# Attention jobs of a hybrid transformer kernel: full-array matmuls, streamed values, the window bias added on VectorE

## The reference

```python
qa = apply_axial_rope(rms_norm(qa...), cos, sin); ka = apply_axial_rope(rms_norm(ka...), cos, sin)
oa = gqa_attention(qa, ka, va) * silu(za)                 # A: 8 query heads, 2 key heads, head size 64
ob = neighbourhood_attention(qb, kb, vb, rpb) * silu(zb)  # B: 8 heads, window of columns + relative bias
mixed = sigmoid(ga) * (oa @ w_o_attn) + sigmoid(gb) * (ob @ w_o_na)
x = x + mixed @ w_out                                     # p = softmax(q k / 8 [+ bias]), out = p v
```

## Time and profile before

| | us |
|---|---|
| median of 3 runs | 1308.72 (1308.57 to 1310.63) |
| profiled execution | 1306.29 |
| its span | 1304.4 |
| PE / DVE / ACT / POOL busy in the span | 1232.6 / 873.0 / 633.6 / 258.6 |
| granted TensorE clock, mean | 0.978 |
| attention part of layer 0 (first score to last value) | 88.5 to 269.6 |
| attention part of layer 1 | 380.0 to 539.2 |

### The profile page before, as it was taken

The page is one execution under the profiler, slowest core; times in us unless marked ns, Lnnn a source line. Parts: engine busy times, 40 slices in busy tenths (PEclk is TensorE's granted clock), DMA queues, the critical chain, the costliest instruction groups (busy, mean ns, idle before and its releaser), DMA issues.

```text
span 1304.4 us, 23474 instructions
## 1 busy us (share of the span) xinstructions
PE 1232.6 (94%) x9420; PEld 1145.0 (88%) x9420; DVE 873.0 (67%) x1886; ACT 633.6 (49%) x960; POOL 258.6 (20%) x192
## 2 busy tenths in 40 slices
PE   6899997999899999989999999999999999999995
PEld 6888886779888887889999998988889999999995
DVE  5655443477655544687877668967784678777666
ACT  6544442246654443365444455447445465444453
POOL 0054553000055541000000004870066000000000
PEclk9999999899999999999999999999999999999998
DMA  6643313234643244145554554232456454554550
GB/s 231 149 158 117 111 66 81 49 112 168 152 165 118 97 101 94 65 162 210 194 182 157 197 185 178 107 133 92 144 145 164 150 201 165 191 194 146 198 207 33
DMA packets 47980, 188.09 MB, mean 144 GB/s; under 512 B 20856, under 2 KB 24184, under 8 KB 29312
## 3 DMA queue, kind: packets, MB, share of 16 engines
q1 hardware_dynamic: 47872, 186.58, 43.7%
HBM read 185.50 MB, written 1.06 MB: 143 GB/s over the span
## 4 chain that ended last, share of the span: by engine, by line
PE 73%; DVE 12%; DMA 6%; ACT 4%; issue 2%; SPq 2%; POOL 0%; DVEq 0%; ACTq 0%
PE line L1777 43%; PE result L1777 16%; DMA raw<-in_weights 4%; PE result L1927 4%; DVE w_lo L1098 3%; PE score L1879 3%; DMA rel<-in_rpb 2%; SPq L597 2%; PE turn L1900 1%; ACT w_hi L684 1%; PE score L1884 1%; PE score L2046 1%; DVE prod L1623 1%; DVE prod L1334 0%; DVE best L1622 0%
## 5 line engine op out<-in xcount | busy, mean ns | idle before, releaser
L667 POOL TENSOR_TENSOR w_lo<-raw,w_hi 128x512 fp32r<-128x512 f32 x184 | 257.8, 1432 | 669.0 <-ACT w_hi L684 669.0
L684 ACT ACTIVATE w_hi<-raw 128x2048 fp32r<-128x2048 f32 (+2 forms) x178 | 321.4, 1808 | 120.3 <-DMA raw<-in_weights 53.7
L1777 PE MATMUL line<-x_hi,w_hi 128*128 128x256 f32 (+1 forms) x1144 | 340.1, 297 | 15.3 <-DVE x_lo L1141 8.8
L1098 DVE TENSOR_TENSOR w_lo<-raw,w_hi 128x512 fp32r<-128x512 f32 (+2 forms) x528 | 323.3, 659 | 17.0 <-ACT w_hi L684 13.4
L1777 PE MATMUL line<-x_hi,w_lo 128*128 128x256 f32 (+1 forms) x1144 | 329.4, 288 | 0.0
L1777 PE MATMUL line<-x_lo,w_hi 128*128 128x256 f32 (+1 forms) x1144 | 329.0, 288 | 0.0
L1777 PEld LDWEIGHTS line<-x_hi,w_hi 128*128 128x128 f32 x1144 | 220.9, 193 | 27.9 <-issue 19.4
L1777 PEld LDWEIGHTS line<-x_lo,w_hi 128*128 128x128 f32 x1144 | 220.6, 193 | 0.9
L1777 PEld LDWEIGHTS line<-x_hi,w_lo 128*128 128x128 f32 x1144 | 221.0, 193 | 0.0
L1777 PE MATMUL line<-y_hi,w_hi 128*128 128x256 f32 (+1 forms) x688 | 205.1, 298 | 2.5 <-DVE y_lo L1149 1.7
L1777 PE MATMUL line<-y_lo,w_hi 128*128 128x256 f32 (+1 forms) x688 | 197.0, 286 | 0.0
(11 more groups left out here) (298 smaller groups left out, 2212.8 us busy)
## 6 DMA issues: line engine op xcount, KB each, us to landing
raw<-in_weights SPq DMA_DIRECT2D x145, 1024.0 KB, 4.8
raw<-in_weights SPq DMA_DIRECT2D x32, 704.0 KB, 4.0
rel<-in_rpb SPq DMA_DIRECT2D x64, 64.0 KB, 7.1
h<-in_tokens SPq DMA_DIRECT2D x2, 544.0 KB, 6.1
raw<-in_weights SPq DMA_DIRECT2D x2, 512.0 KB, 6.1
rbias<-bias_by_distance SPq DMA_DIRECT2D x8, 128.0 KB, 5.5
out<-wide SPq DMA_DIRECT2D x4, 256.0 KB, 2.2
consts<-in_consts SPq DMA_DIRECT2D x1, 832.0 KB, 6.8
```

The source lines that it names most:

```text
L667: pool.tensor_tensor(w_lo[:, u % CUT, at], raw[:, u % RAW, at], w_hi[:, u % CUT, at].bitcast(F32), ALU.subtract).then_inc(lo_pool, 1)
L684: act.activation(w_hi[:, v % CUT, first:n], raw[:, v % RAW, first:n], ACT.Copy).then_inc(hi_cut, 1)
L1098: dve.tensor_tensor(w_lo[:, u % CUT, at], raw[:, u % RAW, at], w_hi[:, u % CUT, at].bitcast(F32), ALU.subtract).then_inc(lo_cut, 1)
L1777: ins = pe.matmul(bank[:, 0:n], stay, move[:, first + k, 0:n], start=(k, m) == (0, 0), stop=(k, m) == (depth - 1, 2))
```

## The change

- Keys lie zero-padded in tiles of all 128 rows (`ka_half`, `kb` with a tile for each head), so scores use K = 128. Probabilities and value tiles are padded to 3 x 128 keys.
- B's queries are stored in reverse order within a tile, so the bias needs no flip matmul: DVE adds it to the scores in PSUM in the instruction that takes the (negated) maximum; Exp has scale -1.
- `values` has the turned probabilities as stationary operand (128 columns) and streams the 64 columns of `v`; the result is query by head, in one of two banks. DVE divides it by the sum there (64 columns in place of 272) and writes it to `head_out`; when both halves of a pair and tile are in, one transpose (`pair_out`) turns them to feature order. The jobs' order has the halves innermost.
- ACT alone copies the turned probabilities (384 columns).
- The walk is three steps longer (`TAIL`); steps 3, 7, 11, ... of the early part have no filler (six in layer 0, three in layer 1).
- The bias is loaded by head pair and query tile (4 DMAs) into a ring of 4; the later four chunks stand behind units that `rel_unit` picks.
- `rot` works on the raw line with the gain folded into its matrix (`rot_gain`); the norm is multiplied in last. `rot` moves to even lines.
- The dummy Ln that brought in an activation table becomes a load of a set by name.

```diff
-    a = [("A", c, half, t) for c in range(PAIRS) for half in range(2) for t in range(TILES)]
-    b = [("B", c, half, t) for c in range(PAIRS) for half in range(2) for t in range(TILES)]
+    a = [("A", c, half, t) for c in range(PAIRS) for t in range(TILES) for half in range(2)]
+    b = [("B", c, half, t) for c in range(PAIRS) for t in range(TILES) for half in range(2)]
...
+TAIL = 3
...
+def filler_at(i):
+
+    steps = len(JOBS[i]) + TAIL
+    blank = steps - len(FILLERS)
+    free = {3 + 4 * n for n in range(blank)}
+    at = [t for t in range(steps) if t not in free]
+    return {t: f for f, t in enumerate(at)}
...
+BIASES = [(c, t) for c in range(PAIRS) for t in range(TILES)]
+RING = 4
...
+def rel_unit(i, n):
+
+
+    c, t = BIASES[n - RING]
+    step = JOBS[i].index(("B", c, 1, t)) + 2
+    f = max(f for s, f in FILLER_AT[i].items() if s <= step)
+    return UNIT[(f"layer{i}", *FILLERS[min(f + 3, len(FILLERS) - 1)])] + RAW
...
+    single_bank = [stat_bank, result_bank[1]]
+    pair_bank = result_bank[0]
...
+    ka_half = a1.sb("ka_half", [2, TOK])
+    kb = a1.sb("kb", [HEADS, TOK])
+    head_out = a1.sb("head_out", [2, P])
     va = a1.sb("va", [3, P])
     vb = a1.sb("vb", [3, HEADS * HD])
-    rel = a1.sb("rel", [2, TILES, 2, SEQ])
+    rel = a1.sb("rel", [RING, 2, TOK])
+    rot_gain = a1.sb("rot_gain", [2, P])
...
-        def load_rel(i, c):
-
-
-            n = PAIRS * i + c
-            if n >= 2:
-
-                sp.wait_ge(score_done, SCORE[(f"layer{(n - 2) // PAIRS}", "B", (n - 2) % PAIRS, 1, TILES - 1)] + 1)
+        def load_rel(i, n):
+
+            k = len(BIASES) * i + n
+            c, t = BIASES[n]
+            if k >= RING:
+
+                j, (c0, t0) = (k - RING) // len(BIASES), BIASES[(k - RING) % len(BIASES)]
+                sp.wait_ge(maxed, JOB[j] + JOBS[j].index(("B", c0, 1, t0)) + 1)
             for half in range(2):
-                for r in range(ROWS):
-                    at = ((i * HEADS + 2 * c + half) * RPB_R + 7 - r) * RPB_C + WIN - GRID_W
+                for odd in range(2):
+                    at = ((i * HEADS + 2 * c + half) * RPB_R + 7 - 2 * t - odd) * RPB_C + WIN - GRID_W
                     src = bass.AP(rpb.tensor, at, [[1, GRID_W], [RPB_C, ROWS], [1, GRID_W]])
-                    dst = rel[(1 - r % 2) * GRID_W:(2 - r % 2) * GRID_W, n % 2, r // 2, half]
-                    sp.dma_start(dst.rearrange("p (r c) -> p r c", c=GRID_W), src).then_inc(rel_in[n % 2], 16)
+                    dst = rel[(1 - odd) * GRID_W:(2 - odd) * GRID_W, k % RING, half, 0:SEQ]
+                    sp.dma_start(dst.rearrange("p (r c) -> p r c", c=GRID_W), src).then_inc(rel_in[k % RING], 16)
...
-                for c, behind in enumerate((5, 6, 22, 24)):
-                    if u == STAGES[f"layer{i}"] + behind:
-                        load_rel(i, c)
+                for n in range(RING):
+                    if u == STAGES[f"layer{i}"] + 5 + n // 2:
+                        load_rel(i, n)
+
+                for n in range(RING, len(BIASES)):
+                    if u == rel_unit(i, n):
+                        load_rel(i, n)
...
+        pool.memset(prod2[:, :, TOK:3 * P], 0.0).then_inc(set_up, 1)
+        pool.memset(probs[:, :, TOK:3 * P], 0.0).then_inc(set_up, 1)
+        pool.memset(ka_half[:, :, :], 0.0).then_inc(set_up, 1)
+        pool.memset(kb[:, :, :], 0.0).then_inc(set_up, 1)
+        pool.memset(rel[:, :, :, SEQ:TOK], 0.0).then_inc(set_up, 1)
...
-            act.activation(warm[:, :], eps[:, :], ACT.Ln)
+            act.preload_act_table_set("natural_log_exp_and_others")
...
+                act.activation(probs[0:m, n % 2, 0:TOK], score_bank[s % 2][0:m, 0:TOK], ACT.Exp,
+                               bias=top[0:m, n % 2, 0:1], scale=-1.0 if job[0] == "B" else 1.0,
+                               accum_out=total[0:m, n % 4, 0:1]).then_inc(exped, 1)
...
-            def head_norm(n):
-                dst = ka[:, :] if n == 0 else qa[:, n - 1, 0:W]
-                g = operand(f"k_gain{i}") if n == 0 else q_gain[:, i:i + 1]
-                r = rstd_of((name, "head", n), W if n else TOK)
-                dve.scalar_tensor_tensor(dst, dst, g, r, ALU.mult, ALU.mult).then_inc(normed, 1)
...
+                dve.wait_ge(raw_head, 5 * i + n + 1)
+                dve.scalar_tensor_tensor(prod[:, 0, 0:w], dst, g, const("cos")[:, 0:w], ALU.mult, ALU.mult)
                 dve.wait_ge(rot_done, 5 * i + n + 1)
                 dve.tensor_tensor(prod[:, 1, 0:w], result_bank[RESULT[key] % 2][:, 0:w], const("sin")[:, 0:w],
                                   ALU.mult).then_inc(rot_used, 1)
                 dve.wait_ge(rot_used, 5 * i + n + 1)
-                dve.tensor_tensor(dst, prod[:, 0, 0:w], prod[:, 1, 0:w], ALU.add).then_inc(roped, 1)
-                if n and w == TOK:
+                link(dve.tensor_tensor(prod[:, 0, 0:w], prod[:, 0, 0:w], prod[:, 1, 0:w], ALU.add))
+                r = rstd_of((name, "head", n), w)
+                if n == 0:
+                    low_, high_ = half_rows(0), half_rows(1)
+                    dve.tensor_tensor(ka_half[low_, 0], prod[low_, 0, 0:w], r[low_], ALU.mult)
+                    dve.tensor_tensor(ka_half[high_, 1], prod[high_, 0, 0:w], r[high_], ALU.mult).then_inc(roped, 1)
+                    return
+                dve.tensor_tensor(dst, prod[:, 0, 0:w], r, ALU.mult).then_inc(roped, 1)
...
+                    bank = line_wait((name, kind, c))
+                    for half in range(2):
+                        r = half_rows(half)
+                        ins = dve.tensor_tensor(kb[r, 2 * c + half], bank[r, 0:TOK], scale[r, 0:TOK], ALU.mult)
+                    ins.then_inc(kq_ready, 1)
...
+                if job[0] == "B":
+
+                    k = len(BIASES) * i + BIASES.index((job[1], job[3]))
+                    dve.wait_ge(rel_ready, k + 1)
+                    dve.tensor_tensor_reduce(bank[:, 0:TOK], bank[:, 0:TOK], rel[:, k % RING, job[2]], scale=-1.0,
+                                             scalar=3.0e38, op0=ALU.add, op1=ALU.min,
+                                             accum_out=top[:, n % 2, 0:1]).then_inc(maxed, 1)
+                    return
...
+            def normal_of(job, n):
...
+                one, half = SINGLE[(i, job)], job[2]
+                if one // 2 >= 2:
+                    dve.wait_ge(paired, one // 2 - 1)
+                dve.wait_ge(valued, n + 1)
+                link(dve.reciprocal(share[:, n % 4, 0:1], total[:, n % 4, 0:1]))
+                dve.tensor_scalar(head_out[:, one // 2 % 2, half * HD:half * HD + HD],
+                                  single_bank[one % 2][:, 0:HD], share[:, n % 4, 0:1], None,
+                                  ALU.mult).then_inc(normal, 1)
...
-                pe.wait_ge(normed, 5 * i + n + 1)
-                pe.matmul(bank[:, 0:src.shape[-1]], const("rot"), src, start=True, stop=True).then_inc(rot_done, 1)
+
+                pe.wait_ge(raw_head, 5 * i + max(n + 1, 3))
+                pe.wait_ge(rot_gain_ready, 2 * i + 2)
+                pe.matmul(bank[:, 0:src.shape[-1]], rot_gain[:, min(n, 1)], src, start=True,
+                          stop=True).then_inc(rot_done, 1)
...
-                    kind, c, half, t = job
-                    r = slice(half * HD, half * HD + HD)
-                    q, k = (qa, ka[r, :]) if kind == "A" else (qb, kb[r, c])
-                    ins = pe.matmul(s[:, 0:TOK], q[r, c, t * P:(t + 1) * P], k, start=True, stop=kind == "A")
-                    if kind == "B":
-
-                        m = PAIRS * i + c
-                        pe.wait_ge(rel_ready, m + 1)
-                        ins = pe.matmul(s[:, 0:SEQ], const("flip"), rel[:, m % 2, t, half], start=False, stop=True)
+                    _, c, half, t = job
+                    ins = pe.matmul(s[:, 0:TOK], qb[:, c, t * P:(t + 1) * P], kb[:, 2 * c + half], start=True, stop=True)
                 ins.then_inc(score_done, 1)
 
...
+                    kind, c, half, t = job
+                    one = SINGLE[(i, job)]
+                    if one >= 2:
+                        pe.wait_ge(normal, one - 1)
+                    if metas_to(i, n - JOB[i]):
+                        pe.wait_ge(gated, (1, 1, 1, 2)[metas_to(i, n - JOB[i])])
+                    head = half if kind == "A" else 2 * c + half
+                    v = (va if kind == "A" else vb)[:, :, head * HD:(head + 1) * HD]
+                    for kt in range(3):
+                        ins = pe.matmul(single_bank[one % 2][:, 0:HD], tn[:, kt * P:(kt + 1) * P],
+                                        v[:, kt], start=kt == 0, stop=kt == 2)
...
+            def pair_out(job):
+
+                if (i, job) not in PAIRED:
+                    return
+                pair, (kind, c, _, t) = PAIRED[(i, job)], job
+                if t == 0 and (kind, c) != ("A", 0):
+                    pe.wait_ge(pair_gated, KT * i + PAIRS * (kind == "B") + c)
+                pe.wait_ge(normal, 2 * pair + 2)
```

(66 more changed lines are left out.)

216 lines of the change are left out of this document (104 added, 112 removed).

## The result

The changed kernel takes 1222.57 us (median; 1218.25 to 1226.14) against 1308.64 for the kernel before on the same chip: ratio 0.9351, interval 0.9322 to 0.9379. The forecast was 1231. The profiled execution spans 1216.1 us, 88.3 less than before. One fp32 matmul of the program shows as two in a trace (a transpose as one), so x2 is one score, and x6 the three value matmuls of a job.

A forecast was written before the change was run, and what follows sets the result against it. TensorE was taken to bound the kernel (busy 1232.6 of 1304.4 us). Savings of 49 + 18.9 + 5.6 + 2.0 + 2.0 = 77.5 from 1306.29 gave 1228.8, plus 2.4 for the median: 1231, range 1221 to 1257.

The forecast's parts named there:

- Matmul time: Attention loop: cheaper scores and values save 0.56 us in each A job, 0.99 in each B job; 49 us taken.
- The values: Attention loop: six value matmuls go from 0.94 to 0.72 us, with 0.06 a job for the transpose; net 0.16.
- The 0.20 for going back from 64 rows: Attention loop: the line behind a 64-row score pair pays 0.20 us for the array's return to 128 rows.
- Late bias stops: B jobs: TensorE stops behind late bias loads vanish, 14.1 us in layer 0 and 4.8 in layer 1, together 18.9.
- Rival 1: Bias loads stay in the way: the 18.9 us stay, the head's 5.6 is lost, time 1256 us; chance 18%.
- Head parts: Before attention: `rot` no longer waiting for the norm gives 5.6 us over both layers, the first head sum 2.0.
- its way to come out lower: Head parts: full clock granted throughout (5.6 us), and more gained at the start, would bring the time towards 1222 us.
- The net 2.8 of each layer: Head part: `vb0` starts 4.9 us earlier, up to 2.8 may be lost at half clock; 2.8 net taken per layer.
- Table loads: Norms: the load between Ln and Exp goes, saving 1.3 us at the last norm and 0.7 in the mixer; 2.0.
- Rival 2: Table loads and head gain nothing, as load insertion may keep its own set for Ln: 1241 us; chance 12%.
- DVE, taken 0.5: B jobs: fused bias addition and maximum on DVE takes 0.5 us, bounds 0.43 and 0.87, hidden beside TensorE's work.
- Rival 3: Attention loop turns DVE-bound and the kernel gets slower, about 1320 us if the fused operation takes 5; chance 4%.

The follow-up runs named there:

- the layout alone: Bias tile rows 272 columns apart and new DMA order, in the kernel before with one table set preloaded: 1277.76 us, ratio 0.9766, against 0.9952 without the layout.

## Why the prediction was right, and where it was not

**Matmul time, forecast 49: right, a little low.** A job after the change takes, beside its turn, 0.46 + 2.84 + 0.62, half of the pair transpose's 0.11 and half of the 0.05 by which every second score is longer: 4.00. Before, an A job took 0.65 + 3.04 + 0.94 = 4.63, a B job 0.65 + 0.63 + 2.84 + 0.94 = 5.06. That gives 32 x 0.63 + 32 x 1.06 = 54, and the attention stretches without the bias term agree: 72.5 - 18.9 = 53.6. A and B steps have become alike, as forecast: in layer 1's steps with a full line the scores start 4.25 and 4.40 us apart by turns, 4.33 on the mean, where I had said 4.4. The values were the mis-sized term: 0.62 for six, where I had read 0.72 from the earlier trace rows. The next group of six in that same view was nearer, 882.21 - 881.62 = 0.59:

```profile
881.62 0.78 PE L2082 MATMUL result<-gate_q,states 128*128 128x64 f32 x6
```

That the weight loads set their pace was right (with 128 columns streamed instead of 64 the six took 0.67 and not 0.62). That the gain came from halving the streamed columns was not: that part is 0.05, and 0.27 came with the full form, without the three changes of form in the rows above. No run changed the padding and the operands' places one by one. The 0.20 for going back from 64 rows was right (64-row scores put back: 19 to 24 us).

The rows had only one 64-row score in each step, and I priced no other order. Two 64-row scores issued together do run at once: 0.66 us for two against 0.65 for one. In this kernel that is worth 0.05 us for two jobs, because the switch of mode takes the rest (3.05 against 2.84 for the line behind), and the order that it needs costs more.

**Late bias stops, forecast 18.9: size right, cause half right.** Leaving these loads out of the kernel before gives 19, and the changed kernel has no stop there. I put all of it down to smaller groups wanted later. But the layout alone, in the old groups and with the old order of jobs, takes 6.4 + 5.7 us off the two attention stretches; the long waits of DVE for a late bias go from three (4.05, 3.30 and 5.05 us) to one of 1.80. What the smaller groups and the later demand do is at most the rest; no run shows them alone. Rival 1 fell: in the changed kernel one of DVE's waits for a bias is long (4.8 us), and PE doesn't feel it.

**Head parts, forecast 5.6 + 2.0, measured 10.8 + 8.4: the weakest step.** It was "PE then runs into the weights held up by the 16 bias DMAs, as these don't move", with a stop of 2 to 4 us before `vb0`. There is no such stop. The DMAs didn't move, but they got cheaper. ACT's timeline after shows the weight cut behind the second group at 55.71; the one that answers to it was at 64.09 before:

```profile
47.74 1.92 ACT L767 ACTIVATE w_hi<-raw 128x2048 fp32r<-128x2048 f32 x1 [5.48 <-DMA raw<-in_weights]
...
55.71 1.92 ACT L767 ACTIVATE w_hi<-raw 128x2048 fp32r<-128x2048 f32 x1 [5.22 <-DMA raw<-in_weights]
```

Of the 19.2, layout gives 6.1 + 5.9, the table set 2.9 + 1.1, and 1.8 + 1.4 are left for the raw rotary turn and the rest. Part of it is clock: over the head parts the granted clock was 0.94 in both layers before and 1.00 in both after, and PE was busy 4.7 + 4.3 us less there. The forecast had named the clock as its way to come out lower. I had credited the raw rotary turn with 5.6; `rot` was where PE happened to stand, and the weights were late whatever it did. What the raw turn would give in the kernel before, with the slow loads, wasn't run. The net 2.8 of each layer wasn't worked out from rows either; it was a choice below 4.9. The loss of up to 2.8 at half clock that stands beside it was an estimate without a row; behind the stop of 3.98 the 5.2 us at 0.50 make 2.6. The diff had the cause in plain sight, a tile that grew from SEQ to TOK in its last dimension and a loop in another order, and I priced it at nothing: "the same DMAs".

**Table loads, forecast 2.0: not seen.** They went as forecast between the two activations of the norms, 48 to 21 in all. In the kernel before they cost 6 us (4 to 9), mostly in the layers; in the changed kernel nothing. Rival 2 was right that they are worth nothing there, for another reason: PE was no longer waiting behind them. At the end 0.8 us came of the 1.3; in the mixer nothing that stands out of the doubt of "the rest". No pause stands behind the last load in the trace before the change: it ends at 1296.62 and the next activation starts at 1296.63.

**DVE, taken 0.5: measured 0.44.** Line 1344 of the changed kernel in its trace, the fused operation (CUSTOM_DVE_ANT_0) and the read of the accumulator behind it, with the shortest, the median and the longest in ns and the first and last start in us:

```profile
L1344 DVE CUSTOM_DVE_ANT_0 score<-score,rel x32: 435/442/450, 154.7 to 439.5; 128x272 f32<-128x272 f32 x32
L1344 DVE DVE_READ_ACCUMULATOR2_ANT top<- x32: 133/141/144, 155.0 to 439.9; 128x1 f32 x32
```

The read, 0.14 us, follows each one. Rival 3 was far: even the two-pass form of 0.9 us in each B job is hidden.

**The sum.** 54 for 49, 18.9 as it was, 19.2 for 7.6, and 3.5 lost where 2.0 was to be gained (in "the rest", within its doubt): 88.6 by these terms, 88.3 in the spans, 77.5 forecast. The two errors on the gaining side, 5 and 11.6, point the same way, and the median came 8.4 below the forecast. It lies only 1.6 above the lower end of the range, 1221, and two of the four runs lie below that end. That the rest was 3.5 longer in this execution, and not 2.0 shorter, hid about half of the 11.6; that much of the hit is luck.

## What to carry to other kernels

- Where an engine stops, follow the wait back to what is late before pricing the removal of the waiting instruction. Move the suspected load: if the stop moves with it, the load is the cause. Here it moved from `rot` (3.98 us) to the turn of `vb` (6.62).
- A DMA that is only laid out differently is a change. Read the issue time of such a group in the DMA queue's timeline before and after; here 7.1 us against 5.5 for 8 DMAs was the sign of a change worth some 20 us in the kernel.
- On a loop that TensorE sets, with small matmuls (64 or 128 columns streamed), count weight loads and changes of the array's form before streamed columns (here six matmuls took 0.05 us more with twice the columns, and 0.27 more with the changes of form); and leave DVE and ACT operations alone that lie beside it (here the two-pass form of 0.9 us on DVE in each B job, and 35 us more of ACT in all, changed the time by nothing that could be told).

## What the hardware showed that I had not expected

- The same bias DMAs (64 KB, runs of 256 bytes) were issued in 5.5 us instead of 7.1 (layer 0's first eight) and landed in 5.8 instead of 7.0 us (median of all 64) when the tile's rows stood 272 columns apart and not 256 and the order of the DMAs was another. The changed kernel has the short issue too (5.56), with a median landing of 6.5. The cause is open.
- Two fp32 scores on separate halves of the rows, issued together, took 0.66 us, one alone 0.65.
- Six matmuls of the trace (three in fp32) with 128 stationary columns took 0.62 us with 64 columns streamed and 0.67 with 128. With 64 stationary columns, 128 streamed and the last two on 16 rows, they took 0.94.
